# Five edits to a two-block transformer kernel's instruction order: projection tiles, modulation columns, a transposition, filler matmuls and a gain

## The reference

```python
# block 1
u = rmsnorm(h, norm1_w) * (1 + sc1) + sh1
hq, hf, hi, hg, aq, ak, av = split(u @ w_in)
mix = concat(hgrn2(hq, hf, hi, hg), diff_attention(aq, ak, av)) @ w_out
h = h + g1 * mix
u = rmsnorm(h, norm2_w) * (1 + sc2) + sh2
h = h + g2 * ((silu(u @ w_gate) * (u @ w_up)) @ w_down)
h = rmsnorm(h, final_norm_w)
# block 2
u = rmsnorm(h, norm_mix_g_2) * (1 + sc) + sh
proj = u @ w_in_2          # queries, 6 key/value parts, gates, stick-breaking q/k/v, merge gates
y_a = gated sum of compressed, selected and window attention @ w_proj_a
y_b = stick_breaking(...) @ w_proj_b
h = h + g * ((sigmoid(m0) * y_a + sigmoid(m1) * y_b) @ w_out_2), then a second feed-forward
```

## Time and profile before

| | us |
|---|---|
| median of three runs | 1482.85 |
| the profiled execution, its own time | 1482.98 |
| its span, first to last instruction | 1481.2 |
| PE busy | 1445.4 (98%) |
| DVE busy | 943.0 (64%) |
| ACT busy | 412.6 (28%) |

### The profile page before, as it was taken

How to read it: one execution, slowest core, us unless ns; L and a number is a source line. 1 busy time by engine, 2 the same in 40 slices (tenths; PEclk the granted TensorE clock), 3 DMA queues, 4 the chain that set the end, 5 groups by cost and what they waited for, 6 DMA issues and landing times.

```text
span 1481.2 us, 19386 instructions
## 1 busy us (share of the span) xinstructions
PE 1445.4 (98%) x7210; PEld 1171.4 (79%) x7210; DVE 943.0 (64%) x1681; ACT 412.6 (28%) x840; POOL 94.6 (6%) x75
## 2 busy tenths in 40 slices
PE   6999998999999999999999999999999999999997
PEld 5888866778888888888876777788887888888886
DVE  8888788876766665656566668864555444454443
ACT  5434354331111110103244555511113222221011
POOL 0000000100000000224300000000030000000110
PEclk9999999999999999999999999999999999999999
DMA  9253422435565555433221111122322222223332
GB/s 370 108 182 130 144 97 81 134 128 185 192 204 185 195 184 162 137 116 116 72 71 53 48 44 43 47 96 89 112 85 85 100 85 103 96 99 93 92 93 92
DMA packets 52609, 175.79 MB, mean 119 GB/s; under 512 B 5952, under 2 KB 6336, under 8 KB 52544
## 3 DMA queue, kind: packets, MB, share of 16 engines
q1 hardware_dynamic: 52544, 174.94, 35.2%
HBM read 172.82 MB, written 2.10 MB: 118 GB/s over the span
## 4 chain that ended last, share of the span: by engine, by line
PE 90%; DVE 6%; ACT 2%; issue 1%; DMA 1%; POOL 0%; SPq 0%; ACTq 0%; DVEq 0%
PE bank L660 20%; PE bank L662 20%; PE bank L661 20%; PE bank L1153 7%; PE bank L1173 2%; PE bank L1208 2%; PE bank L1184 2%; PE bank L836 2%; PE bank L834 2%; PE bank L835 2%; PE bank L1007 1%; PE bank L868 1%; PE bank L672 1%; DVE ada L1725 1%; PE bank L674 1%
## 5 line engine op out<-in xcount | busy, mean ns | idle before, releaser
L660 PE MATMUL bank<-uh,wh 128*128 128x512 f32 x808 | 315.8, 391 | 4.8 <-DVE wl L1705 3.6
L661 PE MATMUL bank<-ul,wh 128*128 128x512 f32 x808 | 315.1, 390 | 0.0
L662 PE MATMUL bank<-uh,wl 128*128 128x512 f32 x808 | 315.0, 390 | 0.0
L1703 DVE CAST wh<-wraw 128x1024 fp32r<-128x1024 f32 (+1 forms) x223 | 148.2, 664 | 194.3 <-PE bank L662 176.0
L1705 DVE TENSOR_TENSOR wl<-wraw,wh 128x1024 fp32r<-128x1024 f32 (+1 forms) x223 | 260.6, 1169 | 7.7
L660 PEld LDWEIGHTS bank<-uh,wh 128*128 128x128 f32 x808 | 152.0, 188 | 37.4 <-issue 4.9
L661 PEld LDWEIGHTS bank<-ul,wh 128*128 128x128 f32 x808 | 152.1, 188 | 31.7
L662 PEld LDWEIGHTS bank<-uh,wl 128*128 128x128 f32 x808 | 152.1, 188 | 31.7
L660 PE MATMUL bank<-hh,wh 128*128 128x512 f32 x352 | 137.5, 391 | 0.0
L662 PE MATMUL bank<-hh,wl 128*128 128x512 f32 x352 | 137.0, 389 | 0.0
L661 PE MATMUL bank<-hl,wh 128*128 128x512 f32 x352 | 137.0, 389 | 0.0
(11 more groups left out here) (352 smaller groups left out, 2269.6 us busy)
## 6 DMA issues: line engine op xcount, KB each, us to landing
ada<-in_w_ada_dram SPq DMA_DIRECT2D x96, 512.0 KB, 4.5
wraw<-in_w_in_dram SPq DMA_DIRECT2D x61, 512.0 KB, 3.2
wraw<-in_w_ffn_gate_dram SPq DMA_DIRECT2D x44, 512.0 KB, 3.2
wraw<-in_w_ffn_up_dram SPq DMA_DIRECT2D x44, 512.0 KB, 3.2
wraw<-in_w_ffn_down_dram SPq DMA_DIRECT2D x32, 512.0 KB, 3.4
wraw<-in_w_ffn_down_dram SPq DMA_DIRECT2D x16, 384.0 KB, 3.1
wraw<-in_w_out_dram SPq DMA_DIRECT2D x16, 256.0 KB, 2.8
wraw<-in_w_out_dram SPq DMA_DIRECT2D x8, 512.0 KB, 3.2
```

The lines of the kernel that those rows point to most:

```text
L660: nc.tensor.matmul(bank[:], a, rh[:, k0 + k, :], start=(first and k == 0), stop=False)
L661: nc.tensor.matmul(bank[:], a, rl[:, k0 + k, :], start=False, stop=False)
L662: mm = nc.tensor.matmul(bank[:], b, rh[:, k0 + k, :], start=False, stop=(last and k == nk - 1))
L1703: V.tensor_copy(wh[:, slot, 0:n], wraw[:, slot, 0:n]).then_inc(w_hi, 1)
```

## The change

Five edits. (1) `KV_PARTS` becomes (6, 3, 5, 2, 4), and the transpositions and ACT's copies of the values move ahead accordingly. (2) The modulations of block 1: four fewer in `a1`, one of them ahead of a split instead of behind it, three more in the loop of `da1`. (3) `da_turn` moves behind the first third of the filler. (4) `keep_busy(2)` before `spread` in `norm(2)` becomes `keep_busy(6)`. (5) The gain of `norm(2)` is computed after `down1` instead of before it.

```diff
-        KV_PARTS = (6, 2, 4, 3, 5)
+        KV_PARTS = (6, 3, 5, 2, 4)
...
-        MOD_AFTER = {PH["a1"].u0 + n + 1: [15 + n] for n in range(1, 13)}
-        MOD_AHEAD = {PH["da1"].u0: [28]}
-        MOD_STATES = {PH["da1"].u0 + 1: [29, 30]}
-        for n_ in range(2):
-            MOD_AFTER[PH["da1"].u0 + 2 * n_ + 1] = [31 + n_]
+        MOD_AFTER = {PH["a1"].u0 + n + 1: [15 + n] for n in range(1, 9)}
+        MOD_AHEAD = {PH["a1"].u0 + 13: [24], PH["da1"].u0: [25]}
+        MOD_STATES = {PH["da1"].u0 + 1: [26, 27]}
+        for n_ in range(5):
+            MOD_AFTER[PH["da1"].u0 + n_ + 1] = [28 + n_]
...
                 da_spare(m)
+                fill1(m, False)
                 if 2 <= m < DA_TILES_N + 2:
                     da_turn(m - 2)
-                fill1(m, False)
                 fill1(m, True)
...
             norm(2)
-            keep_busy(2, B[2])
+            keep_busy(6, B[2])
             spread(B[7], rcol, n_col, 2, n_rstd)
...
             turn_tile(0)
+            turn_tile(1)
             kv_unit(3)
+            pe.wait_ge(drain_a, PH["kv2"].a0 + 3)
+            turn_tile(2)
             kv_unit(4)
-            pe.wait_ge(drain_a, PH["kv2"].a0 + 4)
-            turn_tile(1)
...
             for m in range(ATT_TILES + 3):
+                if m == 3:
+                    pe.wait_ge(drain_a, PH["kv2"].a0 + 5)
...
-                if m == 0:
-                    pe.wait_ge(drain_a, PH["kv2"].a0 + 5)
-                    turn_tile(2)
...
             take_tile(0)
+            take_tile(1)
             kv_drain(3)
+            take_tile(2)
             kv_drain(4)
-            take_tile(1)
-            take_tile(2)
...
             ffn("ff1", 0)
-            v.wait_ge(mod_done, 64)
-            v.wait_ge(wf_ok, 3)
+            add_residual("down1", mod1[:, 40:48])
+            split(PH["kc2"].u0 + 1, (PH["kc2"].u0 + 1) % 2)
+            v.wait_ge(mod_done, 96)
             V.scalar_tensor_tensor(gain[:, 2, :], mod2[:, 8:16], 1.0, vt2[:, NORM_A:NORM_A + KT],
                                    op0=ALU.add, op1=ALU.mult).then_inc(wf_ok, 1)
             v.wait_ge(wf_ok, 4)
             V.tensor_tensor(gain[:, 2, :], gain[:, 2, :], wf, ALU.mult).then_inc(gain_ok, 1)
-            add_residual("down1", mod1[:, 40:48])
-            split(PH["kc2"].u0 + 1, (PH["kc2"].u0 + 1) % 2)
```

## The result

The changed kernel takes 1490.3 us (median of five runs, 1490.24 to 1491.9) where the kernel before took 1482.85. The ratio is 1.0054, interval 1.0043 to 1.0065: 8.0 us more, 6.4 to 9.6. The forecast was 1487.6, range 1484.6 to 1490.8. The ratio, which takes all runs of before into account, puts the changed kernel at 1490.9, just beyond that range. The sign held and so did most of the steps; the sum fell short by 3.2 us.

What follows compares the result with a forecast made beforehand. PE, busy 98% of the span, was taken as the bound, so edits count by its holes and added work. Terms -1.1 + 2.4 + 1.1 + 0.7 + 0 + 1.7 = +4.8 us gave 1487.6 us, range 1484.6 to 1490.8.

Steps and rivals of the forecast that it cites:

- Part A: End of `a1`: the state copy comes earlier and closes PE's hole of 1.11 us, a gain of 1.1 us.
- Part B: Loop of `da1`: of three added modulations, two reach PE at 1.20 us each, a loss of 2.4 us.
- Part C: `da1` loop: `da_turn` behind a third of the filler, slower matmul passages and lost cover, a loss of 1.1 us.
- Part D: `norm(2)`: the longer filler, `keep_busy(6)`, delays the spread, a loss of 0.7 us.
- Part E: Gain of `norm(2)` behind `down1`: two short instructions that cost nothing, bounds 0 and 0.4 us.
- Part F: `kv2`: the filler waits for the key tile, now drained last in four ACT instructions, a loss of 1.7 us.
- Rival 1: New holes in step 8 and `kv2` pull the clock down, 1.7 us per fall: 1489.3 or 1491.0; 16%.
- Rival 2: Clock falls disappear as instruction times shift; all three gone wins 5.1 us, 1482.5; 4% in full.
- Rival 3: `da1` loop: slack absorbs DVE's added load, Part B falls to 0: 1485.2; 16% together with Rival 4 and similar.
- Rival 4: The filler of `b2` doesn't wait for the fifth drain, Part F is -0.2: 1485.7; 16% together with Rival 3 and similar.

Runs made afterwards that it cites:

- y2: The kernel before with only the changed tables of modulations (parts A and B): 1485.4 us, ratio 1.0014.
- x5: The changed kernel with the modulation tables as before, the rest changed: 1488.72 us, ratio 1.0041.
- x4: The changed kernel with `da_turn` ahead of the whole filler again, modulations as changed: 1488.75 us, ratio 1.0041.
- x3: The changed kernel with the gain computed ahead of `down1` again and `keep_busy(6)` kept: 1490.93 us, ratio 1.0059.
- x1: The changed kernel with the order of `kv2` as before, all else as changed: 1489.76 us, ratio 1.0043.
- z2: The changed kernel, unchanged, profiled once more: 1492.52 us.
- z3: The changed kernel with 14 filler matmuls in the hole of step 8 of `da1` and 20 in that of step 16: 1489.17 us, ratio 1.0037.
- y1: The kernel before with its table of modulations redrawn (27 ahead of the last split of `a1`, 28 to 36 placed anew): 1478.26 us, ratio 0.9974.

## Why the prediction was wrong

**The terms held.** Part A was put at -1.1 and measured -0.84 (0.27 of the hole stays). Part B: 2.4 put, 2.24 measured, with holes of 0.76 and 1.86 where 0.8 to 0.9 and 1.8 were forecast. Part C: 1.1 put, 0.7 measured; the passages before existing holes shortened them by more than I took off. Part D: 0.7 put, 0.66 measured alone. Part E: 0 put, inside 0 to 0.4, measured 0.92 alone. But as D and E hide each other, together they cost 0.92. Part F: 1.7 put, 1.83 measured. The sum of these, -0.84 + 2.24 + 0.7 + 0.92 + 1.83 = 4.85, is the 4.8 of the forecast. That they agree so well is luck in part: A, B, C and F came out off by 0.26, -0.16, -0.4 and 0.13, and D with E by 0.22, and these cancel.

**The step that failed** is in the sum: it starts from the profiled execution's 1482.98 us with its three falls and adds nothing for falls, so the change in them was put at nothing and weighed only in the rivals. The reason was that I had read three falls in one profile as a property of the kernel; the second profile of the same kernel has two. The runs show in its place that the changed kernel has more of them: its mean granted clock is 0.9922 over 16 executions against 0.9950 over 74. What the medians have beyond the 4.85 is 8.0 - 4.85 = 3.15 us (1.6 to 4.8). In the two first profiles what is beyond it, 3.6 us, is 1.61 for the fall at 218, 1.45 for the fall at 740 instead of 690, and 0.48 of the front stage. Of these the first belongs to the change: its place is the hole that part B makes, and no kernel without that hole has it. The second is a draw, since the kernel before had its fall at 734 in its own second profile. How the 3.15 us of the medians divide between the tables and parts C to F isn't settled: the profiles would give the tables 2.4, y2 and x5 give them 0.5 to 0.7.

**Rival 1** (new holes pull the clock down) had 16% and is the one that came nearest. In step 8 it is borne out: a fall in 5 of 7 profiles with the hole of 1.8 to 1.9 us, in none of nine with 0.5, in neither of the two with the hole filled. It isn't one hole, one fall, for the same hole has the fall or not (x4, y2). In `kv2` it is refuted: none of the nine profiles with the new order has a fall behind its hole. The argument that I brought against it, that holes of 0.52 and 0.69 were passed at 1.00, was read rightly, and none of the nine profiles with a hole of about 0.5 there has a fall in step 8; but it said nothing of a hole of 1.86. The rule named beside it in the forecast (transpositions don't count as activity) isn't settled by these runs.

**Rival 2** (falls disappear) was half right: one fall or another is missing from execution to execution with nothing in the instructions to account for it, as I wrote, but without the change too, so that is no effect of it. **Rival 3** is refuted by L880 to step 8, +2.22 to +2.24 in the seven profiles with the changed tables and an unfilled hole, +0.02 in x5. **Rival 4** by the 1.72 us hole, in every kernel with the new order.

**Part E's size.** The gain was priced by a reciprocal of 0.18 us, and takes 1.23 in all the kernels that have it in the new place. It has two inputs in SBUF and POOL is in the middle of an instruction; x3's reciprocal, with one input, ran at 0.18 in the middle of the same POOL instruction (675.22 to 676.85). The Trainium skill, "SBUF — State Buffer", section "Who interferes with whom", says that a VectorE instruction with two inputs in SBUF contends with a GpSimd instruction that reads SBUF, over a shared port pair that works as an exclusive lock. The trace agrees: end at 677.82 against 677.80. By that rule the price could have been read ahead of the run, from POOL's row: an estimate of some 1.2 us, the time from DVE's start to POOL's end.

**What stays open.** It isn't known what decides, in one execution, which of the places has its fall, nor how much of the loss beyond the 4.85 us belongs to the tables and how much to the rest. Nor is it shown whether the double falls at 734 to 748 (x1, x5, z2, z3; all with parts D and E, none of the ten profiles without both) belong to the change.

## What to carry to other kernels

Profile the same kernel twice before counting anything that comes from the clock: here two executions of one program differed in the number and place of the falls, at 0.15 to 1.7 us each, while the holes ahead of them repeated to 0.01 us. Sum the instruction-level terms without the falls, and then add falls as an expected number with a spread, more of them where the change opens a hole of a microsecond or two in a stretch that is dense. Compare the medians, too, with what the profiles add up to: here that showed that one place, well explained, was not the whole of it. And where VectorE is busy 93% of a stretch, an instruction taken out of it, to a place where no other engine waits for it, can be worth up to its length: two of part B's three instructions cost 1.1 us each and the third nothing, and the table redrawn that way (y1) is 3.9 us faster than the kernel before.

## What had not been expected of the hardware

A fall of the granted clock had one size in all eighteen profiles: 1.7 us lost, or 3.4 where two stood in a row. A fall can be nearly free: over a stretch in which PE would wait anyway (the 3.30 us split at 692.83) it costs 0.15 us instead of 1.6, so removing it wins little. Falls of the clock stood behind idle times of PE of 0.94 to 2.87 us, and also where PE was busy throughout, at 64 short matmuls of 32 columns (L1129). An instruction of DVE on 8 columns took 1.23 us beside POOL, and the split of a weight tile 3.30 us (from 697.95, with POOL in two instructions of 4.95 us together from 697.44) where it takes 1.22 elsewhere.
